# Laying the matmul operands of a one-core decoder trunk at addresses set by hand

## The reference

```python
h = rmsnorm(x, norm_mix[0])                       # layer 0, mixer
a = h @ w_pw1 + b_pw1                             # 1024 -> 2048
u = a[..., :d] * sigmoid(a[..., d:])
u = silu(layernorm(causal_dwconv(u, w_dw, b_dw))) # width 31
x = x + u @ w_pw2 + b_pw2

up = rmsnorm(x, norm_ffn[i]) @ w_up               # 1024 -> 2 * 2816, both layers
act, gate = up[..., :D_FF], up[..., D_FF:]
act = causal_dwconv(act, w_dw, b_dw)              # width 3
x = x + (silu(act) * gate) @ w_down               # 2816 -> 1024

x = x + scale * (pooled(h) @ w_grp + b_grp)       # layer 1, mixer: windows 2/4/8/16
out = rmsnorm(x, final_norm)
```

## The kernel before

| tensor | before | after |
|---|---|---|
| h_hi, h_lo | 96, 96 | 0, 64 |
| w_raw, slots 0 and 1 | 96, 96 | 64, 64 |
| w_hi, w_lo of slot 0 | 96, 96 | 0, 64 |
| w_hi, w_lo of slot 1 | 96, 96 | 32, 96 |
| rms, sumsq, sq, act_in, band | 96 | 96 |
| y | 0 | 0 |
| u_hi, u_lo (v_hi and v_lo as u_lo) | 0, 0 | 32, 96 |
| glu_hi, glu_lo (first slot, first tap), diagonals, map_hi, map_lo | 0 | 32 |

## Time and profile before

### The profile page before, as it was taken

How to read it: one execution, slowest core, us unless ns; L and a number is a source line. 1 busy time by engine, 2 the same in 40 slices (tenths; PEclk the granted TensorE clock), 3 DMA queues, 4 the chain that set the end, 5 groups by cost and what they waited for, 6 DMA issues and landing times.

```text
span 1016.1 us, 11441 instructions
## 1 busy us (share of the span) xinstructions
PE 978.8 (96%) x4308; PEld 798.8 (79%) x4308; DVE 595.5 (59%) x751; ACT 389.6 (38%) x581; POOL 1.1 (0%) x24
## 2 busy tenths in 40 slices
PE   5999999699999999999999999999999999999994
PEld 4787877488888888888888888788888888888883
DVE  5999999655666555566434328775566555532333
ACT  6639930543433343333222327443333333322220
POOL 0000000000000000000000000000000000000000
PEclk9999999699999999999999999999999999999997
DMA  6220211012323222322232242222323222223212
GB/s 245 100 83 1 84 44 39 1 42 88 120 83 122 85 83 88 119 83 85 63 108 88 83 143 84 83 83 94 113 83 124 83 83 86 73 94 101 85 57 83
DMA packets 15288, 88.50 MB, mean 87 GB/s; under 512 B 1696, under 2 KB 1824, under 8 KB 8224
## 3 DMA queue, kind: packets, MB, share of 16 engines
q1 hardware_dynamic: 15264, 88.19, 25.3%
HBM read 86.09 MB, written 2.10 MB: 87 GB/s over the span
## 4 chain that ended last, share of the span: by engine, by line
PE 95%; DVE 3%; ACT 1%; issue 1%; DMA 0%; DVEq 0%; SPq 0%; ACTq 0%
PE bank L796 28%; PE bank L797 28%; PE bank L798 28%; PE bank L853 2%; PE bank L854 2%; PE bank L855 2%; PE bank L862 1%; PE bank L895 1%; PE bank L868 0%; DMA x_res<-x 0%; DVE out_sb L787 0%; DVE conv_out L650 0%; PE bank L973 0%; PE bank L978 0%; PE bank L977 0%
## 5 line engine op out<-in xcount | busy, mean ns | idle before, releaser
L796 PE MATMUL bank<-h_hi,w_hi 128*128 128x512 f32 x832 | 326.5, 392 | 12.5 <-DVE w_lo L551 11.0
L797 PE MATMUL bank<-h_lo,w_hi 128*128 128x512 f32 x832 | 324.7, 390 | 0.0
L798 PE MATMUL bank<-h_hi,w_lo 128*128 128x512 f32 x832 | 324.6, 390 | 0.0
L520 DVE TENSOR_TENSOR w_lo<-w_raw,w_hi 128x2048 fp32r<-128x2048 f32 (+2 forms) x89 | 180.2, 2028 | 107.4 <-ACT w_hi L310 105.8
L310 ACT ACTIVATE w_hi<-w_raw 128x2048 fp32r<-128x2048 f32 (+2 forms) x88 | 148.8, 1695 | 212.6 <-PE bank L798 212.6
L796 PEld LDWEIGHTS bank<-h_hi,w_hi 128*128 128x128 f32 x832 | 156.9, 189 | 46.7 <-issue 13.0
L797 PEld LDWEIGHTS bank<-h_lo,w_hi 128*128 128x128 f32 x832 | 156.9, 189 | 32.9 <-issue 0.7
L798 PEld LDWEIGHTS bank<-h_hi,w_lo 128*128 128x128 f32 x832 | 156.8, 188 | 32.7
L797 PE MATMUL bank<-u_lo,w_hi 128*128 128x512 f32 x416 | 164.9, 396 | 0.0
L796 PE MATMUL bank<-u_hi,w_hi 128*128 128x512 f32 x352 | 139.1, 395 | 0.0
L798 PE MATMUL bank<-u_hi,w_lo 128*128 128x512 f32 x352 | 139.0, 395 | 0.0
(11 more groups left out here) (122 smaller groups left out, 810.7 us busy)
## 6 DMA issues: line engine op xcount, KB each, us to landing
w_raw<-w_up SPq DMA_DIRECT2D x44, 1024.0 KB, 4.9
w_raw<-w_down SPq DMA_DIRECT2D x32, 704.0 KB, 4.1
w_raw<-w_pw SPq DMA_DIRECT2D x11, 1024.0 KB, 5.5
x_res<-x SPq DMA_DIRECT2D x4, 512.0 KB, 8.8
out<-out_sb SPq DMA_DIRECT2D x8, 256.0 KB, 2.5
w_raw<-w_pw SPq DMA_DIRECT2D x2, 512.0 KB, 7.2
w_raw<-w_pool SPq DMA_DIRECT2D x2, 512.0 KB, 3.5
band_raw<-band SPq DMA_DIRECT2D x1, 800.0 KB, 5.4
```

What stands on the lines that cost most here:

```text
L520: V.tensor_tensor(w_lo[s][:, 0:columns], w_raw[s][:, 0:columns], as_f32(w_hi[s][:, 0:columns]), SUB).then_inc(w_split[s], 1)
L796: M.matmul(dst, a, hi, start=start, stop=False)
L797: M.matmul(dst, a, lo, start=False, stop=False)
L798: return M.matmul(dst, b, hi, start=False, stop=stop)
```

## The change

A constant `LINE = 128` and a helper `phase(want)`, which moves the next free address up to the next one that is `want` past a multiple of 128. It is called ahead of `h_hi`, `h_lo`, each `w_hi` and `w_lo`, `u_hi` and `u_lo`. The two weight slots are now laid out as w_hi0, w_lo0, w_hi1, w_lo1, where they were w_hi0, w_hi1, w_lo0, w_lo1. No instruction is added, removed or moved; they differ in their addresses only. What lies behind a moved tensor moves with it (the table above).

```diff
+LINE = 128
...
+        def phase(want):
+
+            at[0] += (want - at[0]) % LINE
...
         x_res = place("x_res", [P, KD, T], f32)
+        phase(0)
         H_HI = at[0]
         h_hi = place("h_hi", [P, KD, T], f32r)
+        phase(64)
         H_LO = at[0]
         h_lo = place("h_lo", [P, KD, T], f32r)
         w_raw = [place(f"w_raw{s}", [P, UNIT], f32) for s in range(2)]
-        w_hi = [place(f"w_hi{s}", [P, UNIT], f32r) for s in range(2)]
-        w_lo = [place(f"w_lo{s}", [P, UNIT], f32r) for s in range(2)]
+        w_hi, w_lo = [], []
+        for s in range(2):
+            phase(32 * s)
+            w_hi.append(place(f"w_hi{s}", [P, UNIT], f32r))
+            phase(32 * s + 64)
+            w_lo.append(place(f"w_lo{s}", [P, UNIT], f32r))
...
         y = place("y", [P, 2, T], f32)
+        phase(32)
         U_HI = at[0]
         u_hi = place("u_hi", [P, KF, T], f32r)
+        phase(96)
         U_LO = at[0]
         u_lo = place("u_lo", [P, KF, T], f32r)
```

## The result

The changed kernel takes 1026.79 us (median of 4 runs, 1026.77 to 1027.42), the kernel before 1017.22 us beside it (4 runs). The ratio is 1.0093, 95% interval 1.0079 to 1.0108: slower by 9.6 us, where 4.5 us faster was forecast. The time lies inside the stated range, but the sign is wrong.

The account below looks back on a forecast made before the run. TensorE's matmul count times interval bounds the kernel. Up-projection and pw1 slot 1 (-1.0) plus down-projection slot 1 (-3.5) give -4.5 us, others 0: 1011.6 us span, 1013.0 us forecast; range 995 to 1034 us.

Parts of the forecast that it names:

- their bound of 4.5 us: VectorE and ScalarE: address effects lie under the matmuls; without that cover they would cost at most 4.5 us.
- the down-projection's 6.7 ns: Down-projection matmuls take 233.3 ns against the up-projection's 226.7; the prediction put this down to operand addresses.
- modulo 128: All matmuls: moving operand's start minus start of weights loaded meanwhile, modulo 128, decides the interval; the forecast's one choice.
- slot 0 of the up-projection: Up-projections and pw1, slot 0, 1248 matmuls: difference stays 0, so no change in time.
- the down-projection's slot 1: Down-projections, 528 matmuls: difference goes from 32 to 0, gaining 6.7 ns each, -3.5 us; other bound nothing.
- Its slot 0: Down-projections, slot 0, 528 matmuls: difference stays 32, so no change in time.
- -32: Up-projections and pw1, slot 1, 1248 matmuls: difference goes from 0 to -32, -1.0 us; other bound +8.3 us.
- d is the same for all three passes: Matmul triples: moving-minus-weights difference stays equal across passes, since both lo tensors lie 64 behind their hi.
- The rival of the lost beat: Matmuls with h lose 226.7 ns and go to 233: slower, 1022 to 1034 us; chance 40 in 100.
- Its first ground: For the lost beat: after a stop and in taps 231 to 233.3 ns looks ordinary, 226.7 special to one layout.
- Its second ground: For the lost beat: everything with the moving operand at 96 is fast, everything with it at 0 slow.
- The large gain from 64 bytes apart: Rival: 64-byte steps between hi and lo save 6.7 ns, 11.1 plus 4.7 us, giving 997 us; chance 17 in 100.

Follow-up runs that it names:

- The first experiment: Changed kernel with h, both weight slots and u, hi and lo, all at 224 modulo 256; 1009.11 us, ratio 0.9913 to the kernel before.
- The fourth experiment: Changed kernel with hi and lo alike; modulo 256 h at 224, weight slot 0 at 96, slot 1 at 224, u at 32; 1022.01 us.
- the second experiment: Changed kernel with h, both weight slots and u, hi and lo, all at 0 modulo 256; 1009.42 us.
- the third experiment: Changed kernel with all hi parts (h, both weight slots, u) at 0 and all lo parts at 64 modulo 256; 1024.76 us.
- the fifth experiment: Changed kernel, modulo 256: h_hi 0, h_lo 64; slot 0 weights both 0; slot 1 w_hi 0, w_lo 64; u both 0; 1024.46 us.

## Why the prediction was wrong

**Right: what bounds the kernel.** An edit of addresses acted through the interval of the matmuls alone; the waits stayed, and VectorE's and ScalarE's busy times changed by 0.1 us each, so their bound of 4.5 us was not used at all. (The 4.4 us named there as the next longest wait are two waits together, the longest of 3.8 us; nothing hangs on it.)

**Right: the down-projection's 6.7 ns are a matter of addresses.** The first experiment moved u to the others' remainder (the order in which the weight slots lie is that of the change, their remainders are those of before), and got them.

**Wrong: the period, "modulo 128".** The prediction named this as its one choice. By it slot 0 of the up-projection kept its difference of 0; modulo 256 it went to 128. The fourth experiment has 232.5 ns there. In the change that is 1248 matmuls at +5.6 ns, some 7 us where I put nothing, and the down-projection's slot 1 likewise went to 128 and not to 0: 528 x (232.1 - 233.3) = -0.6 us instead of -3.5. Its slot 0, where I also put nothing, gained 528 x 2.1 = 1.1 us.

**Wrong: "-32" from line 1003.** I took 118.3 against 120.0 ns at 256 columns as a sign of what 512 columns do. At 512 columns -32 costs 233.1 ns, +6.4 and not -0.9. After the change line 1003's successor, with a difference of 192, takes (634.53 - 633.85) / 6 = 113 ns, less than either, while 192 at 512 columns gave 233.3, one of the worst:

```profile
633.85 0.28 PE L1016 MATMUL bank<-band,map_lo 128*128 128x256 f32 x1
...
634.53 0.28 PE L1016 MATMUL bank<-band,map_lo 128*128 128x256 f32 x1
```

The first two experiments bring `band` and the maps to one remainder, and there line 1016 takes 120 ns. The second one, six matmuls:

```profile
618.12 0.28 PE L1016 MATMUL bank<-band,map_lo 128*128 128x256 f32 x1
...
618.84 0.28 PE L1016 MATMUL bank<-band,map_lo 128*128 128x256 f32 x1
```

So the two widths rank the differences in another order: 0 is the fastest of all at 512 columns, and at 256 columns it is slower than 192. In the changed kernel slot 1 has 231.5 ns: 1248 x 4.8 = 6 us where I put -1.0 and had +8.3 as the bound.

**Wrong: "d is the same for all three passes" as all that counts.** It was the same, but the third and the fifth experiment show that the short interval also ends when the remainders change from pass to pass. Even with a difference of 0 in every stretch, the 64 bytes between hi and lo gave 231 ns in the third experiment. Slot 0 of the up-projection was thus lost on two counts, and repairing the period alone would not have saved it.

**The rival of the lost beat was the right one**, with both slots lost at 5 to 6 ns instead of 6.7. Its first ground was right: after a stop and in the taps some 231 to 233 ns is what an ordinary pair of addresses gives, and 226.7 what one special layout reaches. Its second ground (the moving operand at 96) fell with the second experiment. What I should have seen is that h and its weights, all at equal remainders, were the only long stretches of fp32r matmuls of 512 columns so laid out, and that the change gave this up. The large gain from 64 bytes apart doesn't exist; it goes the other way from 226.7.

The rule of the Trainium skill that the prediction cites (SBUF — State Buffer, "Who interferes with whom": two independent read ports, and "PE and ACT never wait on anyone") doesn't hold here if it is read as a statement on time. The moving operand's and the weights' addresses relative to each other move the interval from 226.7 to 234.1 ns.

What stays open is the mechanism. All runs agree with the two reads, of the moving operand and of the next weights, getting in each other's way, since moving either of them alone ends the short interval; but no run here takes the weight load away, and what lies between 213.3 and 226.7 ns wasn't reached by any layout. Nor is it tested which weights the moving operand must agree with. If it is the weights already in use, the third experiment has differences of 0, 64 and 192 in turn and not 0 throughout, and then constancy would matter only because it keeps both differences at 0. The average of these three is (226.7 + 229.1 + 233.3) / 3 = 229.7 ns, or 231.2 with the other value of 64, and 231.1 was measured. In the mixed stretches of the fifth experiment such averages come out 2 ns or more too low by either pairing, so the runs don't decide between the two. The taps were not brought to equal remainders; their moving operand shifts by 4 bytes a tap, and by an estimate from 6.7 ns each the 306 of them could give 2 us.

## What to carry to other kernels

Where matmuls of 512 fp32r columns are the bound and each loads its own weights, lay the moving operands and all weights at one remainder modulo 256 and keep it through every pass; here that is worth 0.9% over a layout in which one of two operand sets was off, and 1.7% over one that spread them on purpose. It does not carry over to 256 columns, where equal remainders gave 120 ns and a difference of 192 gave 113. Read the start-to-start interval of each stretch, slot by slot, since the shown durations hide it. When one layout in a trace is faster than all others, first ask what makes it special, before taking the others as neighbours on a scale.

## What the runs showed of the hardware

Interval of a 512-column fp32r matmul at a granted clock of 1.00 (2.4 GHz) against the difference modulo 256, hi and lo at one remainder, measured in the up- or down-projection (-16 and -4 are 240 and 252):

| difference | -16 | -4 | 0 | 4 | 16 | 32 | 48 | 64 | 96 | 128 | 160 | 192 | 224 |
|---|---|---|---|---|---|---|---|---|---|---|---|---|---|
| ns | 233.1 | 232.3 | 226.7 to 227.3 | 233.3 | 227.6 to 228.3 | 233.3 | 231.8 | 229.1 to 229.4, and 233.5 | 233.2 | 232.5 | 234.1 | 232.8 to 233.5 | 233.1 |

I had not expected the period of 256 bytes, nor that equal remainders, which look like the worst case for two reads at once, are the best, nor that the interval depends on what came before. After a stop it takes about eight matmuls to fall into the 226.7 ns, and with a difference of 64 the same addresses gave 229 or 233.5 ns from one half chunk to another.
